# A three-block transformer kernel on one core: the even mixer takes its banded branch first and rotates the axial branch on GpSimd, and the recurrent stage's weight units are cut in two halves

## What is computed

```python
def even_mixer(h, w_in, q_gain, k_gain, sink, w_out, rope1, rope_axial):
    qa, ka, va, qb, kb, vb = jnp.split(h @ w_in, cuts, axis=-1)     # 512,128,128,512,128,128 columns
    qa = apply_axial_rope(rms_norm(qa, q_gain), *rope_axial)
    ka = apply_axial_rope(rms_norm(ka, k_gain), *rope_axial)
    oa = global_gqa(qa, ka, va)                      # 8 heads, every key
    qb, kb = apply_rope(qb, *rope1), apply_rope(kb, *rope1)
    ob = windowed_gqa_sink(qb, kb, vb, sink)         # 8 heads, |q - k| <= 128, one sink per head
    return jnp.concatenate([oa, ob], axis=-1) @ w_out
```

## Time and profile before

| | us |
|---|---|
| median of 3 runs | 1454.11 (1446.38 to 1455.18) |
| the profiled execution | 1452.13, of which the span of instructions is 1450.3 |
| TensorE busy | 1379.7, 95% of the span |
| VectorE busy | 925.5 (64%) |
| ScalarE busy | 657.5 (45%) |
| GpSimd busy | 150.5 (10%) |
| mean granted TensorE clock | 0.965 of full speed |
| even mixer, from its first unit to its third output unit | 206 to 319 |
| recurrent stage, first unit to the first `gated` | 1053.9 to 1207.7 |

### The profile page before, as it was taken

The page is one execution under the profiler, slowest core; times in us unless marked ns, Lnnn a source line. Parts: engine busy times, 40 slices in busy tenths (PEclk is TensorE's granted clock), DMA queues, the critical chain, the costliest instruction groups (busy, mean ns, idle before and its releaser), DMA issues.

```text
span 1450.3 us, 22862 instructions
## 1 busy us (share of the span) xinstructions
PE 1379.7 (95%) x9133; PEld 1265.1 (87%) x9133; DVE 925.5 (64%) x1254; ACT 657.5 (45%) x847; POOL 150.5 (10%) x143
## 2 busy tenths in 40 slices
PE   6999999899999999999999899999789898899996
PEld 6999987689999999999988799999688887799995
DVE  5655566778555575555655566555769548776667
ACT  5434353655434354334554554343355333354552
POOL 1100004018100000000033400000022300000000
PEclk9999999999999999999999899999989879899998
DMA  7755543226655546655454156555334223455550
GB/s 242 229 176 191 185 145 117 84 60 197 204 174 193 182 153 202 195 175 194 150 178 130 46 182 197 186 180 196 116 118 138 96 73 122 140 196 181 176 199 30
DMA packets 164308, 229.42 MB, mean 158 GB/s; under 512 B 3923, under 2 KB 133202, under 8 KB 164128
## 3 DMA queue, kind: packets, MB, share of 16 engines
q1 hardware_dynamic: 162064, 221.33, 47.1%
q0 software_dynamic: 2192, 7.39, 1.8%
HBM read 227.65 MB, written 1.05 MB: 158 GB/s over the span
## 4 chain that ended last, share of the span: by engine, by line
PE 88%; DVE 7%; ACT 2%; issue 1%; POOL 1%; DMA 0%; DVEq 0%; ACTq 0%; POOLq 0%
PE ps L341 28%; PE ps L342 27%; PE ps L343 27%; PE ps L1090 1%; PE ps L1924 1%; DVE w_lo L283 1%; PE ps L1722 1%; PE ps L496 1%; PE ps L381 1%; PE ps L382 1%; PE ps L383 1%; DVE x_tok L1426 0%; ACT w_hi L275 0%; DVE x_tok L1425 0%; POOL p_sb L1180 0%
## 5 line engine op out<-in xcount | busy, mean ns | idle before, releaser
L283 DVE TENSOR_TENSOR w_lo<-raw,w_hi 128x2048 fp32r<-128x2048 f32 x208 | 485.2, 2334 | 175.9 <-ACT w_hi L275 175.8
L341 PE MATMUL ps<-h_hi,w_hi 128*128 128x256 f32 x1936 | 552.3, 285 | 0.5 <-DVE h_lo L619 0.3
L342 PE MATMUL ps<-h_hi,w_lo 128*128 128x256 f32 x1936 | 550.4, 284 | 0.0
L343 PE MATMUL ps<-h_lo,w_hi 128*128 128x256 f32 x1936 | 550.3, 284 | 0.0
L275 ACT ACTIVATE w_hi<-raw 128x2048 fp32r<-128x2048 f32 x208 | 397.2, 1912 | 275.2 <-PE ps L343 275.1
L341 PEld LDWEIGHTS ps<-h_hi,w_hi 128*128 128x128 f32 x1936 | 374.2, 193 | 4.5 <-issue 2.2
L342 PEld LDWEIGHTS ps<-h_hi,w_lo 128*128 128x128 f32 x1936 | 374.3, 193 | 1.8
L343 PEld LDWEIGHTS ps<-h_lo,w_hi 128*128 128x128 f32 x1936 | 374.1, 193 | 0.0
L341 PE MATMUL ps<-w_hi,gu_hi 128*128 128x512 f32 x400 | 156.2, 391 | 0.0
L342 PE MATMUL ps<-w_hi,gu_lo 128*128 128x512 f32 x400 | 156.2, 391 | 0.0
L343 PE MATMUL ps<-w_lo,gu_hi 128*128 128x512 f32 x400 | 155.6, 389 | 0.0
(11 more groups left out here) (285 smaller groups left out, 1509.4 us busy)
## 6 DMA issues: line engine op xcount, KB each, us to landing
raw<-in_ffn_w_up_dram SPq DMA_DIRECT2D x44, 1024.0 KB, 5.4
raw<-in_ffn_w_down_dram SPq DMA_DIRECT2D x44, 1024.0 KB, 4.9
raw<-in_ffn_w_gate_dram SPq DMA_DIRECT2D x43, 1024.0 KB, 5.4
raw<-in_w_up_dram SPq DMA_DIRECT2D x22, 1024.0 KB, 5.1
raw<-in_w_in_dram SPq DMA_DIRECT2D x14, 1024.0 KB, 5.3
raw<-in_odd_w_qkv_dram SPq DMA_DIRECT2D x12, 1024.0 KB, 5.2
raw<-in_w_down_dram SPq DMA_DIRECT2D x11, 1024.0 KB, 4.9
raw<-in_even_w_in_dram SPq DMA_DIRECT2D x6, 1024.0 KB, 5.3
```

The lines of the kernel that those rows point to most:

```text
L283: dve.tensor_tensor(w_lo[slot][:, :], raw[slot][:, :], w_hi[slot][:, :].bitcast(F32), ALU.subtract).then_inc(w_lo_ready, 1)
L341: mm(o, ahi, bhi, start=first, stop=False)
L342: mm(o, alo, bhi, start=False, stop=False)
L343: return mm(o, ahi, blo, start=False, stop=last)
```

## The change

1. Even mixer: the chunks are loaded in reverse, so that the banded branch (with both values) is complete after unit 3. `window` rotates it, token block 0 on VectorE, block 1 on GpSimd, and it is transposed between the two halves of unit 5. The values are split and the first output-weight unit is split ahead of unit 4.
2. The axial branch comes second. GpSimd does both token blocks of its rotation and the scaling by the roots; VectorE does only the sums of squares and the roots, behind attention step 2, together with the split of the second output-weight unit. `("turn", 1)` stays after step 6.
3. The heads run in the other order; the probabilities of the axial heads, now steps 8 to 15, are scaled by GpSimd. `keep_warm` gives 2 matmuls in steps 8 to 13 and none in 14 and 15. The first output unit goes from behind step 15 to behind step 14. The load of the relative bias goes ahead of the rotation on GpSimd's queue.
4. Recurrent stage: `feat_unit` and `tok_unit` can emit one half of a unit, and every unit becomes `("first", n)` and `("second", n)` with small work between. ScalarE and VectorE do the splits and reads of a unit at `second`. The chunks are reordered (QR before QA and KA, the fox values VA directly ahead of IR), and `level_mm` 0 to 3 come earlier.

```diff
-        def feat_unit(pe, n, bank, i=0, ready=None, between=None):
+        def feat_unit(pe, n, bank, i=0, ready=None, between=None, parts=(0, 1)):
...
-            pe.wait_ge(w_lo_ready, 3 * i + (n + 1))
-            for t in range(2):
+            if 0 in parts:
+                pe.wait_ge(w_lo_ready, 3 * i + (n + 1))
+            for t in parts:
...
-            last.then_inc(w_released, 1)
+            if 1 in parts:
+                last.then_inc(w_released, 1)
...
+            def window(self, eng, link, tb):
+
+                self.proj.wait_read(eng, 2)
+                eng.wait_ge(self.tables_ready, 1)
+                t1, t2 = self.products(eng, link, 1, tb, tb)
...
+            def pool_axial(self, pool):
+
+                self.proj.wait_read(pool, 3)
+                pool.wait_ge(self.rope[0], TB)
+                for tb in range(TB):
+                    t1, t2 = self.products(pool, plink, 0, tb, tb)
+                    plink(pool, pool.tensor_tensor(t1, t1, t2, ALU.add))
+                pool.wait_ge(self.roots, 1)
+                for tb in range(TB):
...
-                       [rec_feat(FR, 0, 6, 0, 12), rec_feat(FR, 1, 7, 0, 12),
-                       rec_feat(QA, 0, 6, 1, 0, fox_q_lo), rec_feat(KA, 0, 7, 2, 4, fox_k_lo),
-                       rec_feat(QR, 0, 6, 3, 8), rec_feat(QR, 1, 7, 4, 8),
-                       Tok(VA, 6, 6, V_hi[:, :, 0:512], fox_v_lo),
-                       rec_feat(QA, 1, 6, 7, 0, fox_q_lo), rec_feat(KA, 1, 7, 7, 4, fox_k_lo), Tok(IR, 6, 9, V[:, :, 512:1024]),
+                       rec_feat(QR, 0, 6, 1, 8), rec_feat(QR, 1, 7, 2, 8),
+                       rec_feat(QA, 0, 6, 3, 0, fox_q_lo), rec_feat(KA, 0, 7, 4, 4, fox_k_lo),
+                       rec_feat(QA, 1, 6, 5, 0, fox_q_lo), rec_feat(KA, 1, 7, 6, 4, fox_k_lo),
+                       Tok(VA, 6, (7, 8), V_hi[:, :, 0:512], fox_v_lo), Tok(IR, 6, 9, V[:, :, 512:1024]),
                        Tok(GR, 6, 10, hg_gate)])
...
-        EVEN = [("unit", n) for n in range(3)] + [("rows", 0), ("unit", 3), ("rotate", 0), ("unit", 4), ("unit", 5), ("turn", 0)] \
-            + att(0, 7) + [("turn", 1)] + att(7, 8) + [("split", 0)] + att(8, 9) + [("split", 1)] + att(9, 16) \
-            + [("out", 0)] + att(16, 19) + [("out", 1)] + att(19, 23) + [("out", 2), ("out", 3)]
+        EVEN = [("unit", n) for n in range(3)] + [("rows", 0), ("unit", 3), ("window", 0), ("values", 0), ("split", 0),
+                ("unit", 4), ("first", 5), ("turn", 0), ("second", 5), ("squares", 0)] \
+            + att(0, 3) + [("split", 1), ("roots", 0)] + att(3, 7) + [("turn", 1)] + att(7, 15) + [("out", 0)] \
+            + att(15, 19) + [("out", 1)] + att(19, 23) + [("out", 2), ("out", 3)]
...
-        REC = [("unit", 0), ("unit", 1), ("unit", 2), ("fox_gates", 0), ("fox_z", 0), ("fox_chain", 0), ("gates", 0),
-               ("unit", 3), ("k", 0), ("fox_turn", 0), ("unit", 4), ("fox_wide", 0), ("fox_wide", 1),
...
+        REC = [("first", 0), ("second", 0), ("first", 1), ("fox_gates", 0), ("second", 1), ("fox_z", 0), ("first", 2),
+               ("fox_chain", 0), ("gates", 0), ("second", 2), ("first", 3), ("k", 0), ("second", 3), ("silu_q", 0),
+               ("fox_turn", 0), ("first", 4), ("fox_wide", 0), ("chunks", 0), ("second", 4), ("diag", 0), ("fox_wide", 1),
+               ("first", 5), ("mm64", 0), ("read64", 0), ("fox_wide", 2), ("second", 5), ("mm128", 0), ("read128", 0),
+               ("fox_wide", 3), ("level", 0),
...
+               ("first", 8), ("fox", 2), ("second", 8), ("fox", 3), ("level_mm", 2), ("level_read", 2), ("level", 3),
+               ("first", 9), ("fox", 4), ("second", 9), ("level_mm", 3), ("level_read", 3), ("level", 4),
+               ("first", 10), ("fox", 5), ("second", 10), ("fox", 6), ("first", 11), ("level_mm", 4), ("level_read", 4),
+               ("level", 5), ("fox", 7), ("second", 11), ("fox", 8), ("first", 12), ("fox", 9), ("second", 12), ("fox", 10),
+               ("level_mm", 5), ("level_read", 5), ("first", 13), ("fox", 11), ("fox", 12),
+               ("fox_out", 0), ("rec_mm", 0), ("second", 13), ("gated", 0), ("silu_gate", 0), ("rec_sums", 0), ("split", 1),
...
-                    elif 8 <= n < 16:
-                        keep_warm(pe, 3)
+                    elif 8 <= n < 14:
+                        keep_warm(pe, 2)
```

More of the change, by code:

```diff
@@ L387, in feat_unit_first, with tok_unit @@
             last.then_inc(w_released, 1)
-        def tok_unit(pe, n, half, banks, ready=None, done=None, between=None):
+        def tok_unit(pe, n, half, banks, ready=None, done=None, between=None, parts=(0, 1)):
             slot = n % RING
-            pe.wait_ge(w_lo_ready, n + 1)
+            if 0 in parts:
+                pe.wait_ge(w_lo_ready, n + 1)
             a, b = tok_view(w_hi[slot]), tok_view(w_lo[slot])
-            for tb in range(TB):
+            for tb in parts:
                 for k in range(4):
@@ L1228, in dve @@
                     self.dve_inverse(dve, s - 2)
-                    if not self.causal and not self.by_pool:
+                    if not self.causal and not self.by_pool(s - 2):
                         self.scale(dve, s - 2)
@@ L1938, in build @@
         ODD_NEEDS = {0: 2, 4: 4, 5: 5, 8: 7, 12: 9}
-        REC = [("unit", 0), ("unit", 1), ("unit", 2), ("fox_gates", 0), ("fox_z", 0), ("fox_chain", 0), ("gates", 0),
-               ("unit", 3), ("k", 0), ("fox_turn", 0), ("unit", 4), ("fox_wide", 0), ("fox_wide", 1),
-               ("unit", 5), ("fox_wide", 2), ("fox_wide", 3), ("silu_q", 0), ("chunks", 0),
-               ("unit", 6), ("diag", 0), ("fox", 0), ("unit", 7), ("mm64", 0), ("read64", 0), ("fox", 1),
-               ("unit", 8), ("mm128", 0), ("read128", 0), ("level", 0), ("fox", 2), ("fox", 3),
-               ("unit", 9), ("level_mm", 0), ("level_read", 0), ("level", 1), ("fox", 4),
-               ("unit", 10), ("level_mm", 1), ("level_read", 1), ("level", 2), ("fox", 5), ("level_mm", 2), ("level_read", 2), ("level", 3), ("fox", 6), ("unit", 11), ("fox", 7), ("level_mm", 3),
-               ("level_read", 3), ("level", 4), ("fox", 8), ("fox", 9), ("level_mm", 4), ("level_read", 4),
-               ("level", 5), ("unit", 12), ("fox", 10), ("fox", 11), ("level_mm", 5), ("level_read", 5), ("fox", 12),
-               ("fox_out", 0), ("rec_mm", 0), ("unit", 13), ("gated", 0), ("silu_gate", 0), ("rec_sums", 0), ("split", 1),
@@ new lines, in build @@
+        REC = [("first", 0), ("second", 0), ("first", 1), ("fox_gates", 0), ("second", 1), ("fox_z", 0), ("first", 2),
[3 more added lines that the diff above has]
+               ("fox_wide", 3), ("level", 0),
+               ("first", 6), ("fox", 0), ("second", 6), ("level_mm", 0), ("level_read", 0), ("level", 1),
+               ("first", 7), ("fox", 1), ("second", 7), ("level_mm", 1), ("level_read", 1), ("level", 2),
+               ("first", 8), ("fox", 2), ("second", 8), ("fox", 3), ("level_mm", 2), ("level_read", 2), ("level", 3),
[4 more added lines that the diff above has]
+               ("fox_out", 0), ("rec_mm", 0), ("second", 13), ("gated", 0), ("silu_gate", 0), ("rec_sums", 0), ("split", 1),
@@ L2023, in _ @@
             even_turn.tables(pool)
-            even_turn.pool(pool)
             load_rel(0)
+            even_turn.window(pool, plink, 1)
+            even_turn.pool_axial(pool)
+            for s in range(23):
+                att_even.pool(pool, s)
             pool.wait_ge(att_even.out_ready, 16)
@@ L2092, in _ @@
             for what, n in EVEN:
-                if what == "unit":
+                if what in ("unit", "second"):
                     even_in.act(act, n, split=n < 4)
@@ L2096, in _ @@
                     split_hi(act, even_out.u0 + n)
-                elif what == "rotate":
+                elif what == "values":
+                    even_turn.act_values(act)
+                elif what == "squares":
                     even_turn.act_squares(act)
@@ L2121, in _ @@
             for what, n in REC:
-                if what == "unit":
+                if what == "second":
                     rec_in.act(act, n, split=n < 13)
@@ L2174, in _ @@
                     split_lo(dve, even_out.u0 + n)
-                elif what == "rotate":
-                    even_turn.dve_rotate(dve)
+                elif what == "window":
+                    even_turn.window(dve, dlink, 0)
+                elif what == "values":
+                    even_turn.dve_values(dve)
+                elif what == "roots":
+                    even_turn.dve_roots(dve)
                 elif what == "turn":
@@ L2253, in _ @@
                     even_in.pe(pe, n)
+                elif what == "first":
+                    even_in.pe(pe, n, (0,))
+                elif what == "second":
+                    even_in.pe(pe, n, (1,))
                 elif what == "rows":
@@ L2294, in _ @@
             for what, n in REC:
-                if what == "unit":
-                    rec_in.pe(pe, n)
```

(4 more changed lines are left out.)

153 lines of the change are left out of this document (73 added, 80 removed).

## The result

Medians of 20 runs each: 1457.91 us for the changed kernel (1449.96 to 1464.61), 1452.13 for the kernel before (1446.09 to 1457.51; one execution of it, with 2238 us, was slow and is left out of the ratio). The ratio is 1.0045, 95% interval 1.0029 to 1.0061: some 6.5 us slower. I had said 1450 and a gain of 5; the time lies inside my range of 1439 to 1462 because that was 23 us wide, and the sign was wrong. The profiled execution took 1461.26 us, with a span of 1459.5, 9.2 us more than that of before.

A forecast was written before the change was run, and what follows sets the result against it. TensorE is busy 95% of the span, so only its idle and half-clock time can be won. Even mixer 2.5 plus recurrent stage 2.6 gave 5.1 us: 1447.0 against 1452.13, stated as 1450 because that execution was below the median; range 1439 to 1462.

The forecast's parts named there:

- even: start of step 1: Even mixer: banded rotation and reads done sooner, spare matmuls at full clock, step 1 at 247.8 instead of 251.23; gain 3.4 us.
- even: stall ahead of step 4: Even mixer: TensorE's step 4 waits for VectorE's chain with split, squares' sums and roots; stall 6.4 us.
- even: half clock behind it: Even mixer: one step at half clock after the new stall ahead of step 4; 2.9 us lost.
- even: old stall and its slow step: Even mixer: the stall before step 8 and its half-clock step go, splits being made elsewhere; gain 3.79 + 2.50 = 6.3 us.
- even: tail: Even mixer, late steps: 12 fewer spare matmuls save 2.8 us, GpSimd's scaling is late by 0.7; gain 2.1 us.
- recurrent stage up to gated: Recurrent stage: fewer half-clock losses against more waits, ending at 1205.6 instead of 1207.7; gain 2.1 us.
- what follows it: After the recurrent stage up to gated: a read made during the last wait; gain 0.5 us.
- The signs that I had named for the profile: Waits of 5 to 8 us near 254 to 261, about 7 near 1083 to 1090, 1 to 3 at fox steps.
- two falls, 9 us at half: Recurrent stage from 1112.6: the clock falls twice, 9 us at half clock, 4.0 us lost.
- 0.44 x 34.4 = 15.1 less for the half clock: Recurrent stage from 1112.6: 15.1 us taken off TensorE's 89.5 busy us, leaving 74.4 us of work at full clock.
- Waits traded for waits: The forecast itself, not a rival: 1445 to 1456 us, chance 0.50.
- the clock that stays down: Rival, recurrent stage from fox step 5: new waits leave TensorE at half clock for 34 us again; 1461 us, chance 0.20.

The follow-up runs named there:

- e5: The changed kernel with 34 spare matmuls instead of 4 behind attention step 3, into the wait at step 4; 1452.18 us, ratio 0.9988.
- e3: The changed kernel with sums of squares and roots moved behind attention step 0, second output-weight split just ahead of the first output unit; 1457.76 us, ratio 1.0035.
- e1: The change to the even mixer alone, with the recurrent stage of the kernel before; 1454.2 us, ratio 1.002.
- e9: Changed even mixer, roots behind step 0, GpSimd's products held until then, second split ahead of first output unit; recurrent stage of before; 1445.28 us, ratio 0.9946.
- e11: The kernel of e9 with 13 spare matmuls ahead of the transposition of the running sums in the recurrent stage; ratio 0.9949.
- e8: The kernel before, with 36 spare matmuls ahead of the recurrent stage and 24 ahead of the last feed-forward net; ratio 0.9996.
- e10: The changed kernel with 28 spare matmuls ahead of unit 4 of the recurrent stage; ratio 1.0031.

## Why the prediction was wrong

By profiles, in us gained, against the kernel before:

```
term                                    predicted   measured
even: start of step 1                      +3.4       +4.5   (246.7 instead of 251.2)
even: stall ahead of step 4                -6.4       -8.4   (the wait itself 7.5)
even: half clock behind it                 -2.9       -4.8   (as e5 shows)
even: old stall and its slow step          +6.3       +6.3 }  step 7 to the third output
even: tail                                 +2.1       +1.6 }  unit: 50.2, now 42.3
recurrent stage up to gated                +2.1       -2.2
what follows it                            +0.5       -1.1
odd mixer (not changed)                     0         -5.2
sum                                        +5.1       -9.3
```

The signs that I had named for the profile all came, and none of the contrary ones: the waits stood where they were predicted. What failed is what the sum makes of them. Of the 14.4 us between the two sums 5.6 are the two terms for the half clock behind waits (1.9 in the even mixer, 3.7 in the recurrent stage), 5.2 the odd mixer, and 2.0 the stall.

- **Even, start and stall.** The start was better than predicted by 1.1 us, and the wait took it back: what VectorE has to do decides when step 4 starts, so a TensorE that comes earlier waits longer. The chain itself was 0.4 us longer. (The old stall, which the prediction puts before step 8, stood before step 9: it is behind the second weight split.)
- **Even, half clock.** The step that failed, at its first place. I took the old kernel's 5.5 us behind a wait of 3.8 as the size for any wait. Behind 7.5 us, and in e3 behind 4.5, it was 11.0 us, 4.8 lost. Of six profiles with the wait of 7.5 five have 10.5 to 11.6 us at half clock behind it; e1's has 6.8.
- **Recurrent stage, first part.** Right: unit 4 at 1090.0 by the old kernel's clock of events (1095.9 less the 5.9 that the kernel was behind), predicted 1089.8; mm128 done at 1112.5, predicted 1112.6.
- **Recurrent stage, from there to gated.** 97.4 us instead of 93.0. The waits were 10.9 instead of 12.0, nearly each in its place: 0.6 at step 0 (predicted 1.6), 0.8 at step 4 (0.4), 2.3 at IR (2.0), 1.5, 1.2 and 1.6 at steps 6, 8 and 10 (1.2, 2.8, 1.3), 2.1 ahead of gated (2.7), and 0.8 at step 7, which I did not have. The half clock was 17.5 us instead of 9, 3.7 more: the same step, failed at its second place ("two falls, 9 us at half"). The work was 1.8 more. In other profiles of this stage the half clock was 7.5 to 18.1.
- **The error underneath** is the term "0.44 x 34.4 = 15.1 less for the half clock": less the 4.0 for the two falls, I gave the change 11 us for a clock that would stay up. The 34 us were no outlier, four of the five profiles of before's stage have 31 to 34 and only e1's has 20; but they hid waits: before's stage is only 2.25 us shorter with 13.1 us less of them. So the price of 0.44 a microsecond was too high where VectorE's loop comes next.
- **The end.** The read that I let the last wait hide did not pay: 3.5 us from the first gated transposition to the projection instead of 2.9, and 0.6 in what follows.
- **The rivals.** None came as written. "Waits traded for waits" was the right mechanism and its balance was off; the one on the other side, the clock that stays down, named the right cause in the wrong place, for most of it fell in the two mixers. Of the 5.2 us in the odd mixer up to 3 may belong to the change, the rest was a draw. The ratio says 6.5 us in all: 4.1 are the recurrent stage with what follows it, 0.4 the even mixer, and some 2 are left, which the odd mixer's means would fill but no run shows by itself.

## What to carry to other kernels

Price a wait with the half-clocked work behind it (here 11.0 us of it, or 4.8 us lost, behind waits of 4.5 and 7.5), and take the half clock's length from several profiles, not from one: the same wait of 7.5 us had 6.8 to 11.6 us of it behind it. In this kernel a microsecond at half clock was worth 0.44 in the even mixer, where TensorE was busy without a break (e5), and 0.17 (2.25 / 13.1) in the recurrent stage, where VectorE's loop came next (e1): look at what the other engine has to do before counting on a better clock. A chain of small VectorE instructions belongs into VectorE's idle time with GpSimd quiet beside it: with this, and one weight split moved, the even mixer went from 112.8 to 104.8 us.

## What I had not expected of the hardware

- The half clock can last longer than the wait that it follows: 11.0 us of full activity behind a wait of 4.46 us (e3), 23 us at 0.50 with TensorE busy for 23.04 of 23.10 in the odd mixer. In the odd mixer's same code it was 7, 13, 18, 20 or 26 us.
- The same even mixer with the same waits, 1.3 us at the longest, stayed at full clock from 250 to 276 us in e9 and had a clock of 0.80 there in e11.
- Filling a wait with matmuls kept the clock in one place (e5) and only put the fall off in three others (e8, e10, e11), there behind idles of 0.5 to 1.3 us.
- VectorE instructions of 0.18 us took up to 1.42 us beside GpSimd, ending with GpSimd's instruction within 0.04 us.
